# Suffix sums of a stick-breaking attention in rounded parts, masks added by the matrix engine, and reordered first loads and norms in a two-block transformer kernel

## The reference, cut to what matters

```python
z = einsum('bqhd,bkhd->bhqk', q, k) * scale      # scores
mask = kpos < qpos
log_one_minus = where(mask, log_sigmoid(-z), 0.0)
suffix = cumsum(log_one_minus, reverse=True) - log_one_minus
log_w = log_sigmoid(z) + suffix
w = where(mask, exp(log_w), 0.0)
out = einsum('bhqk,bkhd->bqhd', w, v)
```

## Time and profile before

| what | value |
|---|---|
| median of 3 runs | 729.43 us (728.14 to 730.09) |
| the profiled execution | 727.93 us, its span 726.2 us |
| PE busy | 719.7 us, 99% of the span |
| DVE, ACT, POOL busy | 488.2, 390.8, 173.1 us |
| granted TensorE clock | 1.00 throughout |

### The profile page before, as it was taken

The page is one execution under the profiler, slowest core; times in us unless marked ns, Lnnn a source line. Parts: engine busy times, 40 slices in busy tenths (PEclk is TensorE's granted clock), DMA queues, the critical chain, the costliest instruction groups (busy, mean ns, idle before and its releaser), DMA issues.

```text
span 726.2 us, 9011 instructions
## 1 busy us (share of the span) xinstructions
PE 719.7 (99%) x3414; PEld 593.4 (82%) x3414; DVE 488.2 (67%) x660; ACT 390.8 (54%) x501; POOL 173.1 (24%) x113
## 2 busy tenths in 40 slices
PE   8999999999999999999999999999999999999998
PEld 7777888888888888888888888888888888888886
DVE  6899999999977555555556446669856565654532
ACT  7546676655884464444444435578745444543330
POOL 1298989989200030000000001142001000000000
PEclk9999999999999999999999999999999999999999
DMA  9876446544476556665655565543264555456540
GB/s 319 258 219 229 151 141 203 193 157 143 174 250 213 175 174 193 194 192 174 190 188 186 176 204 162 186 174 116 80 211 165 182 175 174 174 185 216 178 145 29
DMA packets 83819, 131.57 MB, mean 181 GB/s; under 512 B 4049, under 2 KB 37017, under 8 KB 83777
## 3 DMA queue, kind: packets, MB, share of 16 engines
q1 hardware_dynamic: 82544, 129.74, 54.3%
q10 hardware_dynamic: 1088, 1.06, 0.5%
q0 software_dynamic: 144, 0.20, 0.2%
HBM read 129.75 MB, written 1.25 MB: 180 GB/s over the span
## 4 chain that ended last, share of the span: by engine, by line
PE 95%; DVE 2%; ACT 1%; POOL 1%; DMA 1%; issue 0%; ACTq 0%
PE acc L1689 28%; PE acc L1691 28%; PE acc L1690 28%; PE aux L1366 4%; PE aux L1409 1%; PE acc L1673 1%; PE acc L1681 1%; PE acc L1677 1%; PE aux L1427 1%; ACT w_hi L618 1%; DMA x_t<-xt_dram 1%; PE aux L1455 0%; POOL qk_r L505 0%; POOL rstd L505 0%; DVE w_lo L942 0%
## 5 line engine op out<-in xcount | busy, mean ns | idle before, releaser
L942 DVE TENSOR_TENSOR w_lo<-raw,w_hi 128x2048 fp32r<-128x2048 f32 x96 | 217.6, 2269 | 119.9 <-ACT w_hi L618 119.9
L618 ACT ACTIVATE w_hi<-raw 128x2048 fp32r<-128x2048 f32 (+1 forms) x115 | 218.1, 1900 | 137.3 <-PE acc L1691 136.3
L1689 PE MATMUL acc<-w_hi,h_hi 128*128 128x512 f32 x616 | 245.5, 399 | 0.4 <-DVE tok L1006 0.4
L1691 PE MATMUL acc<-w_hi,h_lo 128*128 128x512 f32 x616 | 240.6, 391 | 0.0
L1690 PE MATMUL acc<-w_lo,h_hi 128*128 128x512 f32 x616 | 240.0, 390 | 0.0
L1689 PEld LDWEIGHTS acc<-w_hi,h_hi 128*128 128x128 f32 x616 | 115.8, 188 | 25.0 <-issue 1.4
L1691 PEld LDWEIGHTS acc<-w_hi,h_lo 128*128 128x128 f32 x616 | 115.6, 188 | 24.7
L1690 PEld LDWEIGHTS acc<-w_lo,h_hi 128*128 128x128 f32 x616 | 115.9, 188 | 22.5
L599 POOL TENSOR_TENSOR w_lo<-raw,w_hi 128x2048 fp32r<-128x2048 f32 x21 | 97.7, 4666 | 1.5 <-ACT w_hi L618 1.5
L995 DVE SCALAR_TENSOR_TENSOR aux<-glu_t,vec_t,aux 128x256 f32<-128x256 f32 x232 | 93.6, 481 | 0.0
L505 POOL TENSOR_TENSOR rstd<-ms,nhalf 128x2 f32<-128x2 f32 x4 | 10.7, 2674 | 323.8 <-DVE ms L976 311.0
(11 more groups left out here) (223 smaller groups left out, 671.3 us busy)
## 6 DMA issues: line engine op xcount, KB each, us to landing
raw<-w_in_dram SPq DMA_DIRECT2D x29, 1024.0 KB, 5.2
...
```

The costliest lines, as they stand in the source:

```text
L618: nc.scalar.activation(w_hi[:, u % SPLIT, 0:nk, :], raw[:, u % RAW, 0:nk, :], ACT.Copy)\
L942: nc.vector.tensor_tensor(w_lo[:, u % SPLIT, 0:nk, :], raw[:, u % RAW, 0:nk, :], f(w_hi[:, u % SPLIT, 0:nk, :]), ALU.subtract).then_inc(w_ ...
L1689: nc.tensor.matmul(o, x_h, w_hi[:, slot, j, :], start=begin_, stop=False)
L1691: mm = nc.tensor.matmul(o, x_l, w_hi[:, slot, j, :], start=False, stop=end_)
```

## The change

1. **Suffix sums.** DVE no longer multiplies with the mask; it rounds the sum into `sp_hi` (fp32r) and puts the rest into `sp_lo`, which lies where `soft` lay, so ACT's `soft` of pair n+2 now waits for the suffix sums of pair n. `suffixes(n)` uses fp32r triangles and squares: for each head two matmuls of 384 columns and two of 128.
2. **Mask by PE.** `scores2(n)` gets one fp32r matmul more for each head, identity by a diagonal block of -1e30, two blocks of 128 columns. `log_weights` becomes a minimum with 0 alone. POOL builds five fp32r constants instead of two masks.
3. **Place of the last sums.** `suffixes(3)` moves from behind unit B+10 to behind the first k-tile of unit B+11.
4. **Start.** x's first two k-tiles come in two transfers with a semaphore each; ACT and DVE handle k-tile 0 of x and of w before k-tile 1 of x.
5. **q's norm.** `TAPS_AT` is 0, 8, 10 at s = 3, 4, 5; the product `norm_qk("q", 0)` stands at s = 4, before `w_lo` of unit 6.

```diff
-    TAPS_AT = {3: 8, 4: 4, 5: 6, 6: 13, ...
+    TAPS_AT = {3: 0, 4: 8, 5: 10, 6: 13, ...
...
-            x_quarter(sp, 0)
+            xt_tiles = a["xt"].rearrange("(k p) s -> p k s", p=P)
+            for kt in range(2):
+                sp.dma_start(x_t[:, kt, :], xt_tiles[:, kt, :]).then_inc(x_first[kt], 16)
...
-            first_stage(0)
+            first_stage(0, (0,))
             first_high(0, 0)
+            first_stage(0, (1,))
             first_high(0, 1)
...
                 if n >= 2:
-                    act.wait_ge(sp_made, n - 1)
+                    act.wait_ge(sfx_done, n - 1)
...
                 dve.wait_ge(sp_made, n + 1)
-                nc.vector.tensor_tensor(w2, w2, again(mask[:, :], 2), ALU.mult).then_inc(sp_ready, 1)
+                if n >= 2:
+                    dve.wait_ge(sfx_done, n - 1)
+                nc.vector.tensor_scalar(hi, w2, 1.0, None, ALU.mult).then_inc(sp_round, 1)
+                dve.wait_ge(sp_round, n + 1)
+                nc.vector.tensor_tensor(lo, w2, f(hi), ALU.subtract).then_inc(sp_ready, 1)
...
-                nc.vector.scalar_tensor_tensor(out=w2_t[:, 2 * n:2 * n + 2, :], in0=aux[:, pair_banks(n), 0:ZC],
-                                               scalar=0.0, in1=again(neg_mask[:, :], 2), op0=ALU.min, op1=ALU.add)\
+                nc.vector.tensor_scalar(w2_t[:, 2 * n:2 * n + 2, :], aux[:, pair_banks(n), 0:ZC], 0.0, None, ALU.min)\
...
+                if s == Q0:
+                    norm_qk("q", 0)
                 if s in (Q0, K1):
                     split_low(s + LEAD)
...
+                for j in range(2):
+                    diag = aux[:, 2 * (n % 2) + j, :].rearrange("p (a b) -> p a b", a=2)[:, :, 0:P]
+                    mm = nc.tensor.matmul(diag, ident_r[:, :], diag_r[:, :, :], start=False, stop=False,
+                                          skip_group_check=True)
...
-                    nc.tensor.matmul(aux[:, bank, 0:S], neg_tri[:, :], sp_[:, 0:S], start=False, stop=False,
+                    for part in (sp_hi[:, n % 2, j, :], lo[:, j, :]):
+                        nc.tensor.matmul(aux[:, bank, 0:ZC], tri_r[:, :], part[:, 0:ZC], start=False, stop=False,
+                                         skip_group_check=True)
+                    nc.tensor.matmul(aux[:, bank, P:S], one_r[:, :], sp_hi[:, n % 2, j, S:ZC], start=False, stop=False,
                                      skip_group_check=True)
...
                 if s == B + 10:
                     suffixes(2)
-                    suffixes(3)
...
+                    if j == 0 and s == B + 11:
+                        suffixes(3)
```

More of the change, by code:

```diff
@@ L183, in build @@
         ff_s = sb("ff_s", [P, NT, 256])
-        mask = sb("mask", [P, ZC])
-        neg_mask = sb("neg_mask", [P, ZC])
+        neg_diag = sb("neg_diag", [P, P])
+        diag_r = sb("diag_r", [P, 2, P], F32R)
+        ident_r = sb("ident_r", [P, P], F32R)
+        tri_r = sb("tri_r", [P, P], F32R)
+        one_r = sb("one_r", [P, P], F32R)
         neg_tri = sb("neg_tri", [P, P])
@@ L239, in build @@
         gelu_t = sb("gelu_t", [P, CT2, S])
-        soft = sb("soft", [P, 2, ZC])
-        soft2 = sb("soft2", [P, 2, ZC])
+        soft, at = place("soft", [P, 2, ZC])
+        sp_lo = sb("sp_lo", [P, 2, ZC], F32R, at=at)
+        soft2, at = place("soft2", [P, 2, ZC])
+        sp_lo2 = sb("sp_lo2", [P, 2, ZC], F32R, at=at)
         assert cursor[0] <= region + 4 * FK2 * S + 8 * NT * 256, cursor[0]
@@ L278, in build @@
         raw_in = [sem(f"raw_in{i}") for i in range(RAW)]
-        x_loaded = [sem(f"x_loaded{g}") for g in range(UK)]
+        x_first = [sem("x_first0"), sem("x_first1")]
+        x_loaded = [None, *(sem(f"x_loaded{g}") for g in range(1, UK))]
         piece_in = [sem(f"piece_in{k}") for k in range(PIECED * UK)]
@@ L571, in _ @@
                     pool.wait_ge(stage_lo, 16)
-                    nc.gpsimd.memset(mask[:, :], 1.0).then_inc(zeros_ready, 1)
-                    nc.gpsimd.memset(neg_mask[:, :], 0.0).then_inc(zeros_ready, 1)
+                    nc.gpsimd.memset(neg_diag[:, :], 0.0).then_inc(zeros_ready, 1)
                     nc.gpsimd.memset(neg_tri[:, :], -1.0).then_inc(zeros_ready, 1)
@@ L624, in first_high, with first_stage @@
                     .then_inc(first_hi if kt < UK - 1 else w_hi_ready, 1)
-            def first_stage(g):
-                act.wait_ge(x_loaded[g], 16)
-                for kt in (2 * g, 2 * g + 1):
+            def first_stage(g, tiles=(0, 1)):
+                if g:
+                    act.wait_ge(x_loaded[g], 16)
+                for kt in (2 * g + j for j in tiles):
+                    if g == 0:
+                        act.wait_ge(x_first[kt], 16)
                     nc.scalar.activation(h_hi[:, kt, :], x_t[:, kt, 0:S], ACT.Copy, scale=x_t[:, kt, S:S + 1])\
@@ L948, in first_low, with first_stage @@
                     .then_inc(first_lo if kt < UK - 1 else w_lo_dve, 1)
-            def first_stage(g):
-                dve.wait_ge(stage_hi, 2 * g + 2)
-                for kt in (2 * g, 2 * g + 1):
+            def first_stage(g, tiles=(0, 1)):
+                for kt in (2 * g + j for j in tiles):
+                    dve.wait_ge(stage_hi, kt + 1)
                     nc.vector.scalar_tensor_tensor(out=h_lo[:, kt, :], in0=x_t[:, kt, 0:S], scalar=x_t[:, kt, S:S + 1],
@@ L1218, in _ @@
                 for kind, i in QK:
-                    if i < 2 and s == end[kind, i] + 1:
+                    if i < 2 and s == end[kind, i] + 1 and s != Q0 + 1:
                         ahead = 0 if (kind, i) != ("q", 1) else min(2, quota[s] - early)
@@ L1445, in scores2 @@
                                      skip_group_check=True)
-                    mm = nc.tensor.matmul(aux[:, bank, S:ZC], k2_t[ps, n, P:S], q2_t[ps, n, P:S], start=False,
-                                          stop=False, skip_group_check=True)
+                    nc.tensor.matmul(aux[:, bank, S:ZC], k2_t[ps, n, P:S], q2_t[ps, n, P:S], start=False,
+                                     stop=False, skip_group_check=True)
+                for j in range(2):
+                    diag = aux[:, 2 * (n % 2) + j, :].rearrange("p (a b) -> p a b", a=2)[:, :, 0:P]
+                    mm = nc.tensor.matmul(diag, ident_r[:, :], diag_r[:, :, :], start=False, stop=False,
+                                          skip_group_check=True)
                 mm.then_inc(z_made, 1)
```

35 lines of the change are left out of this document (18 added, 17 removed).

## The result

The changed kernel takes 731.92 us (median of 5 runs, 731.88 to 732.18), the kernel before 728.14 us (5 runs, 727.78 to 730.09). The ratio is 1.0045, with a 95% interval of 1.003 to 1.006. The forecast was 727.6 with a range of 726.0 to 729.8, so the time lies outside. The profiled execution took 731.91 us, its span is 730.2 us; that of before was 727.93 and 726.2.

A forecast was written before the change was run, and what follows sets the result against it. PE, busy 719.7 of 726.2 us, was taken as the bound. Start -0.4, q's product -0.5 and attention -0.9 gave -1.8 us: 729.43 - 1.8 = 727.6 us, range 726.0 to 729.8.

The forecast's parts named there:

- q's product: Before unit 6: reduce ahead of eight convolution steps, product ends at 37.7, PE's 0.37 us gap closes; -0.5 us (-0.65 to 0).
- k's product: Due for unit 8 on DVE: ended at 50.8, PE needed it at 53.05; 2.2 us slack covers DVE's 1.4 us lateness.
- Behind that, DVE has waits: After unit 8: DVE catches up in waits on PE-made work, first 0.75 us at 82.21; costed at nothing, otherwise up to 0.9 us.
- Start: First matmuls: one `h_hi` is enough, PE starts 0.6 us earlier, k-tile 3's `w_hi` limits the gain; -0.4 us (-0.6 to 0.1).
- set by the bytes ahead of them: Start: the pieces' landing depends on bytes ahead, which don't change, though each is issued some 0.5 us later; supports -0.4 us.
- set by the issue instead: Start, alternative: landing follows the issue, k-tile 3 is half a microsecond late and the gain is nothing.
- Attention: Block 2's attention: sums save 2.6 us of PE, masks cost 1.8; with DVE's changes -0.9 us (-1.1 to +1.35).
- Up to B+10: Attention before unit B+10: all four masks but two of the sums, DVE's roundings disappear in its 1.51 us wait; +0.1 us.
- a square: Suffix sums: an fp32r matmul of 128 columns, taken as 0.11 us; bounds 0.057 and 0.22.
- the rounding: Attention on DVE: rounding 768 elements at two elements a cycle, 0.6 us; upper bound 0.96 us.
- the mask: Attention on PE: a pair's mask costs 0.23 to 0.68 us, including entering and leaving half-row work; 0.45 taken.
- By the same shift: Whole time: the median lies 1.5 us above the profiled execution, so 1.8 us is taken from 729.43.

The follow-up runs named there:

- undoing only the clock: The changed kernel with 32 idle transposes on PE ahead of unit 6's waits, so that the clock can't fall; 732.25 us, ratio 1.0049.
- POOL waits: The changed kernel with one wait more: POOL begins `w_lo` of unit 7 only when DVE has finished that of unit 6; 727.96 us, ratio 0.9990.
- The kernel with k's reduce early: The changed kernel with `w_lo` of unit 6 ahead of q's product and six convolution steps instead of ten ahead of k's reduce; 727.35 us, ratio 0.9979.
- the run with one transfer: The kernel with `w_lo` first and k's reduce early, with x's first two tiles in one transfer again; 726.91 us, ratio 0.9971.
- 20 turns: The kernel before with 20 instead of 16 idle transposes on PE ahead of its first real matmul; 728.06 us, ratio 0.9986.

## Why the prediction was wrong, point by point

- **q's product: the step that failed.** "The next late thing would be `w_lo` of unit 6, now behind the product: 37.7 + 2.2 = 39.9", and with it a gain of 0.5 us. The start (37.8) was right, the duration was not: 6.42 us. PE waited 3.56 us at unit 6 where no wait was forecast, and 4.7 us of loss lie between units 3 and 8. I took the duration from DVE's rows alone and didn't ask what POOL does in that stretch. In the kernel before, DVE's `w_lo` ran from 37.39 to 39.67 and POOL's from 39.67, one behind the other; the change had DVE arrive 0.35 us after POOL had begun. The trace of before also had rows with such a hold. These are POOL, then DVE:

```profile
491.87 4.04 POOL L499 TENSOR_SCALAR w_hi<-raw 128x2048 fp32r<-128x2048 f32 x1 [3.39 <-PE acc L1691]
...
489.47 1.21 DVE L1318 TENSOR_TENSOR decay_gate<-decay 128x1024 f32<-128x1024 f32 x1
...
494.06 2.92 DVE L1325 TENSOR_TENSOR in_gate<-in_gate,lru_tmp 128x1024 f32<-128x1024 f32 x1
```

  The same number of elements takes 1.21 us at 489.47 (and 1.22 with two different tensors at 509.79 in the earlier trace rows), and 2.92 us at 494.06, where POOL is at work until 495.9. The last one ends 1.1 us behind POOL's, as long as it takes alone. The runs with POOL waiting, with POOL's operation halved and with DVE's `w_lo` first showed the mechanism. The Trainium skill states it ("SBUF — State Buffer", SBUF: two separate sides): a DVE operation with two SBUF inputs and a GpSimd operation that reads SBUF take a shared pair of ports exclusively, for the whole instruction. The trace agrees: 6.42 us behind one POOL instruction, 4.27 behind a half. That was a rule that spoke against this change, and the prediction weighed others instead.
- **Unit 8, a step left out.** "k's product, due for unit 8 ... slack of 2.2 us covers this" looked at the accumulator alone. Unit 8's `w_lo` on POOL stood behind k's reduce and power with about 0.1 us of slack. The loss grew from 3.3 us at unit 6 to 4.8 at unit 8; PE's slow matmuls and this chain each account for that by themselves, so undoing only the clock gave nothing. Undoing only the hold (POOL waits) left 1.1 us of waiting at unit 8 by this chain.
- **"Behind that, DVE has waits ... I cost it at nothing."** The kernel with k's reduce early shows 0.40 us at 92.79: nearly the whole gain at unit 6. The bound named there, up to what had just been gained, was closer than nothing.
- **Start: -0.4 forecast, +0.1 measured.** PE started even earlier than forecast (4.91). w's first piece took 3.3 us instead of 3.9. I named k-tile 3's piece as the one that binds, and it came no later than before (9.02 against 9.18). The late ones were k-tiles 1 and 2, `w_hi` starting at 6.25 and 8.12, the latter 0.44 us later than before (7.68). For them the step "set by the bytes ahead of them" was wrong, and "set by the issue instead" right, as the run with one transfer showed; for k-tile 3 the runs don't show it. In this execution PE's first six matmuls also ran at the distance of the 1.2 GHz level and used up the lead of 1.1 us by k-tile 1; with part 5 undone they did not, and the start was still no gain.
- **Attention: -0.9 forecast, -0.8 measured.** The mechanism was right throughout. Up to B+10 +0.15 (forecast +0.1), from there -0.96 (forecast -1.0). A triangle costs 0.175 us (0.17), a square 0.06 and then 0.11 (0.11), the rounding 0.56 (0.6), a pair's sums 1.1 (1.12). A pair with its mask takes 500.45 - 499.16 = 1.29 us against 0.75 before: 0.54 for the mask, where 0.45 was taken. The matmuls that the prediction counts at 0.23 us are less than half of it. DVE's wait of 1.51 us is gone, and `suffixes(3)` at 524.42 comes 0.24 us behind its operand's end (523.22 + 0.96), without a wait.
- **The median.** "By the same shift", 1.5 us from the profiled execution to the median, was no shift. It was the start's second group, as far as the runs show: with 20 turns the kernel before has no such group. A median of three runs fell among the upper ones. The changed kernel's five runs have no upper group, so it is 4.1 us slower than the lower group of before (727.84) and 2.1 us slower than the upper one (729.82).
- **The range.** By its own terms, up to a change of nothing and a spread of 1 us, it should have reached 730.4 and not 729.8; 731.92 lies outside either.
